# Two-layer hybrid encoder: the second layer behind its mixer on 1024 tokens in two blocks of 512

## What is computed

```python
mix = hybrid_mixer(rmsnorm(h, norm_mix_pre[l]), ...)   # ends in concatenate([y_lru, y_gla]) @ w_out
h = h + rmsnorm(mix, norm_mix_post[l])
ff = squared_relu_mlp(rmsnorm(h, norm_mlp_pre[l]), w_up, w_down)   # square(relu(h @ w_up)) @ w_down
h = h + rmsnorm(ff, norm_mlp_post[l])
# at the end: return h[:, N_META:]
```

## Time and profile before

| what | value |
|---|---|
| median of 3 runs | 2413.98 us (2413.72 to 2414.93) |
| the profiled execution's own time | 2414.39 us |
| its span, first to last instruction | 2412.6 us |
| busy: PE, PE weight load, VectorE, ScalarE, POOL | 2371.8, 2303.0, 995.6, 585.7, 752.3 us |
| mean granted TensorE clock | 0.995 of 2.4 GHz |
| DMA | 139.05 MB, mean 58 GB/s |

### The profile page before, as it was taken

How to read it: one execution, slowest core, us unless ns; L and a number is a source line. 1 busy time by engine, 2 the same in 40 slices (tenths; PEclk the granted TensorE clock), 3 DMA queues, 4 the chain that set the end, 5 groups by cost and what they waited for, 6 DMA issues and landing times.

```text
span 2412.6 us, 35076 instructions
## 1 busy us (share of the span) xinstructions
PE 2371.8 (98%) x15144; PEld 2303.0 (95%) x15144; DVE 995.6 (41%) x989; ACT 585.7 (24%) x719; POOL 752.3 (31%) x401
## 2 busy tenths in 40 slices
PE   7999999999999999999999999999999999999996
PEld 6999889999999999999989998899999999999996
DVE  4788543721221221221577974526221221222226
ACT  4464332411011011011336452415010010010012
POOL 2433225033333333333323421240333333333340
PEclk9999999999999999999999999999999999999998
DMA  3111002411111111111331110124111111111123
GB/s 117 44 51 42 27 27 88 132 46 44 44 43 52 43 43 43 52 61 44 97 111 45 37 43 27 37 78 134 44 44 48 48 43 43 52 43 43 50 73 116
DMA packets 57644, 139.05 MB, mean 58 GB/s; under 512 B 4944, under 2 KB 32848, under 8 KB 57552
## 3 DMA queue, kind: packets, MB, share of 16 engines
q1 hardware_dynamic: 28368, 99.20, 12.9%
q10 hardware_dynamic: 29184, 38.49, 5.0%
HBM read 120.57 MB, written 17.10 MB: 57 GB/s over the span
## 4 chain that ended last, share of the span: by engine, by line
PE 93%; DVE 4%; ACT 2%; issue 1%; DMA 0%; POOL 0%; SPq 0%; DVEq 0%; ACTq 0%; POOLq 0%
PE banks L433 78%; PE banks L534 3%; PE banks L477 3%; PE banks L466 1%; PE banks L467 1%; PE banks L480 1%; PE banks L679 1%; PE banks L686 1%; PE banks L635 1%; PE banks L656 1%; PE banks L757 1%; PE banks L694 1%; PE banks L562 0%; DVE qi L1446 0%; PE banks L623 0%
## 5 line engine op out<-in xcount | busy, mean ns | idle before, releaser
L433 PE MATMUL banks<-X,w_hl 128*128 128x348 f32 (+1 forms) x7488 | 1214.4, 322 | 2.2 <-ACT ki L1046 1.8
L433 PEld LDWEIGHTS banks<-X,w_hl 128*128 128x128 f32 x7488 | 1189.1, 188 | 11.5 <-issue 7.8
L347 POOL TENSOR_SCALAR w_hl<-w_raw 128x1024 fp32r<-128x1024 f32 x168 | 192.4, 1145 | 1550.4 <-PE banks L433 803.6
L433 PE MATMUL banks<-act_hi,w_hl 128*128 128x348 f32 (+1 forms) x2880 | 537.2, 321 | 0.0
L349 POOL TENSOR_TENSOR w_hl<-w_raw,w_hl 128x1024 fp32r<-128x1024 f32 x168 | 473.6, 2819 | 14.0
L433 PEld LDWEIGHTS banks<-act_hi,w_hl 128*128 128x128 f32 x2880 | 471.2, 188 | 0.0
L1097 ACT ACTIVATE T<-T 128x1044 f32<-128x1044 f32 x64 | 69.0, 1079 | 1196.6 <-DVE T L1543 1196.6
L1543 DVE SCALAR_TENSOR_TENSOR T<-banks,rs 128x1044 f32<-128x1044 f32 x64 | 79.7, 1246 | 583.8 <-PE banks L433 573.6
L433 PE MATMUL banks<-act_lo,w_hl 128*128 128x348 f32 (+1 forms) x1440 | 306.5, 321 | 0.0
L1564 DVE TENSOR_TENSOR Y<-banks,Y 128x1044 f32<-128x1044 f32 x96 | 119.6, 1245 | 374.4 <-PE banks L433 374.4
L433 PEld LDWEIGHTS banks<-act_lo,w_hl 128*128 128x128 f32 x1440 | 241.3, 188 | 0.0
(11 more groups left out here) (169 smaller groups left out, 1978.5 us busy)
## 6 DMA issues: line engine op xcount, KB each, us to landing
w_raw<-w_units SPq DMA_DIRECT2D x184, 512.0 KB, 3.5
h_mid<-Y ACTq DMA_DIRECT2D x24, 348.0 KB, 4.0
h_out<-Y ACTq DMA_DIRECT2D x24, 348.0 KB, 2.7
Y<-x_in ACTq DMA_DIRECT2D x6, 696.0 KB, 10.1
h_old<-x_in ACTq DMA_DIRECT2D x12, 348.0 KB, 3.5
h_old<-h_mid ACTq DMA_DIRECT2D x12, 348.0 KB, 3.6
h_old<-h_out ACTq DMA_DIRECT2D x12, 348.0 KB, 3.5
X<-h_mid ACTq DMA_DIRECT2D x6, 696.0 KB, 9.1
```

The source lines that it names most:

```text
L347: nc.gpsimd.tensor_scalar(slot[:, 0], w_raw[:, s], 1.0, 1.0, ALU.mult, ALU.mult).then_inc(w_rounded, 1)
L433: ins = nc.tensor.matmul(out[:, b, 0:width(b)], wp, xp[:, used(b)], start=first and n == 0, stop=last and n == 2)
```

## The change

`Tokens` describes a cut of the tokens: number of blocks, their width, the first token and the number of tokens. `FULL` is the old cut, `LAST` is two blocks of 512 from token 16 on. Everything behind the mixer of the second layer takes `LAST`: output projection, both norms, MLP, residuals, loads and stores. All counts of semaphores follow from it. The two tiles (behind the mixer) and four tiles (behind the MLP) by blocks stay, in two blocks now. With `LAST`, pieces are 8 of 512 tokens; `update` on VectorE begins piece 1 behind all sums. The square and residual buffers for pieces of 512 lie in other places. Apart from that, in the first norm of layer 0 VectorE adds the two halves of a piece's squares (`add_halves`), and PE sums them with one ones-matmul for a piece and not two (`sbase == 0` holds there alone). The core of the diff:

```diff
+@dataclass(frozen=True)
+class Tokens:
+    nb: int
+    bn: int
+    first: int
+    n: int
+    @property
+    def pieces(self):
+        return self.nb * QT
+    def cols(self, b):
+        return slice(b * self.bn, (b + 1) * self.bn)
+    def used(self, b):
+        return slice(b * self.bn, min((b + 1) * self.bn, self.n))
+    def width(self, b):
+        return min(self.bn, self.n - b * self.bn)
+    def all(self):
+        return slice(0, self.nb * self.bn)
+    def valid(self):
+        return slice(self.first, self.first + self.n)
+FULL, LAST = Tokens(NB, BN, 0, NT), Tokens(2, 512, N_META, SEQ)
...
+def behind_mixer(l):
+    return LAST if l == L - 1 else FULL
+def of_norm(l, norm):
+    return FULL if norm in (PRE_MIX, NEXT_PRE_MIX) else behind_mixer(l)
...
+        def blk(ap, t=FULL):
+            return ap[:, t.all()].rearrange("p (b n) -> p b n", b=t.nb)
+        def h_old(t, n):
+            return h_old_last[n % 3][:, :, :] if t is LAST else h_old_full[:, n % 3]
+        def sq(t, n):
+            return sq_last[n % SQ_RING][:, :, :] if t is LAST else sq_full[:, n % SQ_RING]
...
-            def product(out, w, xs, first, last):
+            def product(out, w, xs, first, last, t=FULL):
                 for n, (wp, xp) in enumerate(((w[0], xs[0]), (w[0], xs[1]), (w[1], xs[0]))):
-                    for b in range(NB):
-                        ins = nc.tensor.matmul(out[:, b, 0:width(b)], wp, xp[:, used(b)],
+                    for b in range(t.nb):
+                        ins = nc.tensor.matmul(out[:, b, 0:t.width(b)], wp, xp[:, t.used(b)],
                                                start=first and n == 0, stop=last and n == 2)
...
             def add_piece(l, norm, n, sbase):
-                b, first, last = n // QT, n % QT == 0, n % QT == QT - 1
+                t, b, first, last = of_norm(l, norm), n // QT, n % QT == 0, n % QT == QT - 1
                 if first:
                     take_sum_bank(l, norm, b)
+                if sbase == 0:
+                    pe.wait_ge(sq_added, n + 1)
+                    nc.tensor.matmul(sum_bank(l, norm, b), ones[:, :], sq(t, n)[:, 0, :], start=first, stop=last)\
+                        .then_inc(sum_done if last else sq_read, 1)
+                    return
                 pe.wait_ge(sq_h, sbase + n + 1)
-                nc.tensor.matmul(sum_bank(norm, b), ones[:, :], sq[:, n % SQ_RING, 0, :], start=first, stop=False)
-                nc.tensor.matmul(sum_bank(norm, b), ones[:, :], sq[:, n % SQ_RING, 1, :], start=False, stop=last)\
+                nc.tensor.matmul(sum_bank(l, norm, b), ones[:, :], sq(t, n)[:, 0, :], start=first, stop=False)
+                nc.tensor.matmul(sum_bank(l, norm, b), ones[:, :], sq(t, n)[:, 1, :], start=False, stop=last)\
                     .then_inc(sum_done if last else sq_read, 1)
             def first_pair(l, norm, unit, j, slots, xbase, sbase, last_sum):
+                t = of_norm(l, norm)
...
-                for n in range(NX):
+                for n in range(t.pieces):
                     m, b = piece(n)
-                    late = b == NB - 1
+                    late = b == t.nb - 1
...
-                    if n == NX - 1:
+                    if n == t.pieces - 1:
                         first.then_inc(mm_done, 1)
                     for k in lag:
                         lo_pass(1, b, k)
-                    if n == 2 and last_sum:
+                    if n == (2 if t is FULL else 1) and last_sum:
                         row_sum(*last_sum)
                 for k in range(QT, KT):
-                    hi_passes(1, NB - 1, k)
+                    hi_passes(1, t.nb - 1, k)
                 for k in range(QT, KT):
-                    ins = lo_pass(1, NB - 1, k)
...
                 ins.then_inc(mm_done, 1)
             def by_blocks(l, phase, units, slots, xs, sums):
-                late, j0, first_block = LATE[phase], j_late(phase), count(BLOCKS, l, phase)
+                t, late, j0, first_block = behind_mixer(l), LATE[phase], j_late(phase), total(blocks, l, phase)
                 per_unit = late // len(units)
-                for b in range(NB):
+                for b in range(t.nb):
...
-                inv_root(l, norm, 1)
-                squares(2, second)
-                new_piece(3)
+                squares_of(1, second)
                 if last:
-                    log_mean(l, norm, 2)
-                    inv_root(l, norm, 2)
-                    for n in range(4, NX):
+                    root(norm, 1)
+                    for n in range(1, t.pieces):
                         new_piece(n)
+                elif t is LAST:
+                    new_piece(1)
+                    new_piece(2)
+                    root(norm, 1)
+                    new_piece(3)
+                    new_piece(4)
+                    log_mean(l, norm + 1, 0)
+                    new_piece(5)
+                    new_piece(6)
+                    inv_root(l, norm + 1, 0)
+                    new_piece(7)
                 else:
...
+            def add_halves(n):
+                dve.wait_ge(sq_h, n + 1)
+                s = sq(FULL, n)
+                V.tensor_tensor(s[:, 0, :], s[:, 0, :], s[:, 1, :], ALU.add).then_inc(sq_added, 1)
...
                 out(1, second)
-                adds(1, first)
-                new_piece(1)
-                adds(1, second)
-                out(2, first)
-                new_piece(2)
-                out(2, second)
-                adds(2, first)
-                new_piece(3)
-                adds(2, second)
-                for n in range(4, NX):
-                    new_piece(n)
+                sums(1, first)
+                if t is LAST:
+                    sums(1, second)
+                    for n in range(1, t.pieces):
+                        new_piece(n)
+                else:
+                    new_piece(1)
+                    sums(1, second)
+                    out(2, first)
+                    new_piece(2)
+                    out(2, second)
+                    sums(2, first)
+                    new_piece(3)
+                    sums(2, second)
+                    for n in range(4, NX):
+                        new_piece(n)
                 if not last:
-                    split_lo(*next_gain, NX - 1, xbase)
...
             for n in range(NX):
-                split_lo(0, P_GMIX, n, 0)
+                split_lo(0, P_GMIX, n, 0, FULL)
+                add_halves(n)
```

More of the change, by code:

```diff
@@ L862, in squares, with squares_of, root @@
-                def squares(b, us):
+                t, late, norm, last = behind_mixer(l), LATE[phase], POST_MIX + 2 * phase, (l, phase) == (L - 1, 1)
+                def squares_of(b, us):
                     for u in us:
                         square_block(l, phase, b, u)
+                def root(norm, b):
+                    log_mean(l, norm, b)
+                    inv_root(l, norm, b)
                 def new_piece(n):
                     m, b = piece(n)
-                    act.wait_ge(y_new, (l * 2 + phase) * NX + n + 1)
+                    act.wait_ge(y_new, total(pieces, l, phase) + n + 1)
@@ L875, in update @@
+                    act.dma_start(stream(target, n, t), Y[:, m:m + 2, t.cols(b)]).then_inc(h_stored, 16)
                 first, second = range(late // 2), range(late // 2, late)
-                squares(0, range(late))
-                log_mean(l, norm, 0)
-                inv_root(l, norm, 0)
-                squares(1, first)
+                squares_of(0, range(late))
+                root(norm, 0)
+                squares_of(1, first)
                 new_piece(0)
-                squares(1, second)
@@ L1225, in update @@
                 out(0, range(1, late))
-                adds(0, range(late))
+                sums(0, range(late))
                 out(1, first)
```

258 lines of the change are left out of this document (132 added, 126 removed).

## The result

The changed kernel takes **2391.44 us**, the median of 4 runs (2390.95 to 2392.51), against 2414.45 for the kernel before on the same chip: ratio 0.9905, 95% interval 0.9888 to 0.9923. That is 23.0 us less. The forecast was 37.1 less, 2377, with a range of 2360 to 2404. The profiled execution took 2391.31 us, its span 2389.6.

What follows compares the result with a forecast made beforehand. The prediction took TensorE (PE), busy 2371.8 of 2412.6 us, as the bound. Its terms, -36.1 - 0.3 - 6.0 + 2.5 + 2.8 = -37.1 us, gave 2377 us against the median of 2413.98, range 2360 to 2404.

Steps and rivals of the forecast that it cites:

- (a): Second layer behind its mixer: 1728 sweeps of two 512-column matmuls, excess fixed at 14.3 ns each, gain 36.1 us.
- proportional rival: Same fp32r sweeps: the 10% excess grows with the columns, gain 12.6 us instead of 36.1, 2401 us; chance 0.26.
- vanished excess: Same sweeps: the excess goes away with long matmuls, gain 85 us instead of 36.1, 2328 us; chance 0.07.
- slower rival: 512-column fp32r matmuls: cost per column grows faster than the columns, 143 us more, 2518 us; chance 0.04.
- (b): Second layer, sums of squares on PE: fewer, wider fp32 records and row sums, gain 0.3 us.
- (c): First norm of layer 0: VectorE adds halves, PE saves one ones-matmul per piece, net gain 6.0 us.
- (d): Second layer, seam from output projection to MLP: new PE wait of 2.5 us at piece 0's low split.
- (e): Tail after PE's last tile: VectorE's drain, sums, seven wider pieces and last store, 2.8 us lost.
- (f): Inside the MLP: narrower VectorE, ScalarE, POOL work, fewer residual loads, POOL's weight splits, all hidden by PE; no gain.

Runs made afterwards that it cites:

- the matmuls by themselves: Separate kernel, nothing beside PE, stretches of 96 matmuls at several widths and types: fp32r 226.7, 186.7, 158.2, 120.0 ns for 512, 416, 348, 256 columns.
- the four kernels of their own: Separate PE-only kernels computing nothing of the reference: matmul widths and types; shifted activations; weights and activation shifted; rule modulo 256. Unshifted 512-column fp32r: 226.7 ns in the first three.

## Why the prediction was right in sign and range, and high in gain

- **(a), the sweeps: the mechanism was right, the term mis-sized.** "I take the excess as fixed" is what the matmuls by themselves show: 13.2 to 13.4 ns from 256 to 512 columns. The proportional rival falls with it, and the vanished excess and the slower rival fall with 226.7 and 231.2 ns. What failed is that all 14.3 ns were taken as a price that stays the same, and no term was set up for where the operands lie. The changed kernel has 231.2 - 213.3 = 17.9 ns: 13.3 fixed and 4.6 because activation and weights stand at different places modulo 256 bytes. Tiles are 4176 bytes apart there, 80 modulo 256, so one in 16 stands right. The kernel before has 158.7 - 144.4 = 14.3, at most one above 13.3. How much of that one is addresses is not shown: unshifted, two blocks of 348 and one of 344 would take (2 x 158.3 + 157.8)/3 = 158.1. So a sweep went from 476.1 to 462.4 and the term is 13.7 x 1728 = 23.7 us in place of 36.1. With the places put right a sweep takes 453.3, a little under the 455.2 of the forecast. 231.2 is inside the bounds of 222 to 232 under which the forecast was to stand, by less than a nanosecond, and it lies nearer to the 234.4 of the proportional rival than to the 227.6 of the forecast. The time is no better witness: 2391 is 14 above the forecast, at the very end of its own band (2363 to 2391), and 10 under that rival's 2401. That the time still fell in the range is owed to the room that the range had for the rival, so in part to luck. That the fixed excess and not the rival is right comes from the matmuls by themselves; the time could not have told.
- **The slower rival was added up wrongly.** Its 143 us are counted against the kernel before, so it stood for 2414 + 143 - 1 = 2556 us and not 2518. Nothing hangs on it, since both lie outside the range.
- **(b), the sums of squares: as forecast.** The two records of L514 start 0.86 us before L515, 430 ns each.
- **(c), the first norm: 3.6 us in place of 6.0.** The waits for the addition are 1.3 us, as forecast (0.55 at 16.52 and 0.71 later). What was not seen is that the new start keeps the clock down: PE stays at the lower level some 3 us longer, which costs 1.4 us by the comparison above; 1.0 of the shortfall stays unassigned. In the other three traces with that start the lower level ended 0.7 to 1.9 us earlier than in the change's own, so part of the 1.4 is this one execution. That the wait sets it off, and not the one fp32 sum less, is likely but not shown. The timeline of before would have shown a stretch at the lower level, two fp32 sums 1.16 us apart there and 0.58 us apart later:

```profile
16.17 1.36 PE L466 MATMUL banks<-sq,ones 128*128 128x348 f32 x2
17.33 1.37 PE L467 MATMUL banks<-sq,ones 128*128 128x348 f32 x2
```

  Piece 0, which the prediction called PE's, was the first with a wait. With pieces 0 and 1 left to PE the lower level ends as before.
- **(d), the seam: 2.33 us against 2.5**, at the place and for the cause named. **(e), the tail: 2.4 against 2.8.** Sums are 0.79 apart, pieces 2.58, as worked out. Both are an order that can be mended: 4.4 us by the stretches.
- **(f), nothing: as forecast.** No new wait in the MLP; PE is busy all 667.0 us.

With the measured terms: -23.7 - 0.3 - 3.6 + 2.3 + 2.4 = -22.9, and 23.0 were measured. The Trainium skill ("TensorE: Matmul & The Clock Gate", section "Back-to-back issue gap") gives N/2.4 + 2.5 ns. bf16 by itself follows it within 2.2 ns here (213.6 and 146.3, where it gives 215.8 and 147.5); fp32r doesn't, at any width (226.7 where it gives 215.8).

## What to carry to other kernels

Fewer and wider fp32r matmuls save 13 to 15 ns for each one taken away, between 256 and 512 columns. With 512 columns, give the activation tile and the weight tile that stream together the same place modulo 256 bytes: 3456 matmuls from 231.2 to 226.7 ns are 16 us of 2391 here, of which the MLP stretch alone shows 12.8 (644.1 to 631.3), and it costs some padding. When pieces get wider and fewer, write the other engines' order anew, because the last drain now stands in front of more work; and where a stream of matmuls has just begun, half a microsecond of waiting and one fp32 sum less went with some 3 us more at the lower clock level, 1.3 us lost on average here.

## What was not expected of the hardware

- An fp32r matmul costs its columns at 2.4 GHz and 13.3 ns more (14.5 at 344 and 352 columns); a bf16 matmul 0.3 to 1.3 ns more. At the lower level the excess is gone: the first matmuls of 512 columns in the four kernels of their own start 426 to 427 ns apart, which is 512 columns at 1.2 GHz, and those of 348 columns in the change 290. Why was not found.
- fp32r matmuls of 512 columns take 226.7 to 227.2 ns where activation and weights stand at the same place modulo 256 bytes on a multiple of 32, and 228.9 to 236.6 elsewhere; with weights of 64 columns they took 230.0 at the same place. The Trainium skill ("TensorE: Matmul & The Clock Gate", section "Step-by-step: what each phase is for") says that the streamed operand and the weight load have two independent read ports. These stretches ran nothing beside PE, and the time still depends on the one address against the other, which two reads that never meet would not explain. That the two collide in the memory is a reading, not shown. Open stay the values in between (229.0 at 64 bytes, 233.2 at 192), why two equal shifts of 16 bytes cost 233.3, and whether bf16 has it.
- Addresses count at 348 columns too, but less: 158.3 to 160.0 ns by themselves, and 0.7 ns a matmul for act_hi in layer 0 when the tiles moved. The best places there were not looked for, and shifting 344 columns off the same place made them faster, so the rule for 512 may not be theirs.
- In all four traces where PE waits 0.55 us for the first addition and makes one fp32 sum less, it stays at the lower level until 20.5 to 22.3 us; in the six without, until 17.6 to 19.2 us. The granted clock of that stretch reads 1.00 in every one, since a trace has no clock record ahead of the rise.
